# Squares summed on VectorE ahead of one ones-product, and short sequences' new states by 32-row groups

## The reference, cut to what matters

```
k_end = kc * exp(gcum[..., -1:] - gcum)[..., None]
S = S * exp(gcum[..., -1])[..., None, None] + einsum('bhsk,bhsv->bhkv', k_end, u)      # DeltaNet: 4 heads, 128 x 128
...
w_end = exp(gcum[:, -1:] - gcum) * dtc
h = h * exp(gcum[:, -1])[:, :, None, None] + einsum('bsh,bshp,bshn->bhpn', w_end, xc, bc)  # state space: 8 heads, 64 x 128
...
y = y.reshape(bsz, L, MIX_W) * silu(z)
y = y * rsqrt(mean(y * y, axis=-1, keepdims=True) + EPS) * ssd_norm_w      # MIX_W = 512
```

## Time and profile before

| | |
|---|---|
| median of 3 runs | 2747.01 us |
| span of the profiled execution, first to last instruction | 2742.6 us |
| PE busy | 2566.3 us (94%) |
| DVE busy | 1077.8 us (39%) |
| ACT busy | 776.6 us (28%) |
| granted PE clock, mean | 0.981 |

### The profile page before, as it was taken

How to read it: one execution, slowest core, us unless ns; L and a number is a source line. 1 busy time by engine, 2 the same in 40 slices (tenths; PEclk the granted TensorE clock), 3 DMA queues, 4 the chain that set the end, 5 groups by cost and what they waited for, 6 DMA issues and landing times.

```text
span 2742.6 us, 38895 instructions
## 1 busy us (share of the span) xinstructions
PE 2566.3 (94%) x16078; PEld 1550.6 (57%) x16078; DVE 1077.8 (39%) x1748; ACT 776.6 (28%) x1385; POOL 66.4 (2%) x66
## 2 busy tenths in 40 slices
PE   6998999998999999999999999999997899989994
PEld 3555777775555566655555556665446444434443
DVE  4597444544413225553232375752336011101115
ACT  3353323222301111111143118642014122222224
POOL 0000000000000000000000000000000000000003
PEclk9999999999999999999999999999998899999998
DMA  7000122114000011141111210112205656657436
GB/s 307 31 31 34 40 76 102 43 61 158 31 31 31 31 46 57 45 154 63 37 42 50 110 55 33 42 67 120 107 8 197 265 217 241 256 228 287 172 126 223
DMA packets 65269, 291.98 MB, mean 106 GB/s; under 512 B 8956, under 2 KB 32068, under 8 KB 44612
## 3 DMA queue, kind: packets, MB, share of 16 engines
q1 hardware_dynamic: 52996, 255.92, 24.5%
q0 software_dynamic: 8928, 22.03, 2.3%
q10 hardware_dynamic: 3168, 11.54, 1.0%
HBM read 694.20 MB, written 56.63 MB: 274 GB/s over the span
## 4 chain that ended last, share of the span: by engine, by line
PE 81%; DMA 8%; DVE 5%; ACT 4%; issue 2%; SPq 1%; POOL 0%; DVEq 0%; ACTq 0%; POOLq 0%
PE psum L519 30%; PE psum L676 16%; PE psum L1484 8%; DMA arena<-in_moe 6%; PE psum L1342 4%; PE psum L1468 4%; PE psum L1091 2%; PE psum L633 2%; ACT arena L1708 1%; PE psum L537 1%; PE psum L1076 1%; PE psum L563 1%; PE psum L1103 1%; DVE arena L2079 1%; ACT arena L1758 1%
## 5 line engine op out<-in xcount | busy, mean ns | idle before, releaser
L519 PE MATMUL psum<-arena 128*128 128x384 f32 x2544 | 827.1, 488 | 8.1 <-DVEq L321 4.6
L519 PEld LDWEIGHTS psum<-arena 128*128 128x128 f32 x2544 | 485.1, 191 | 347.2 <-issue 9.3
L676 PE MATMUL psum<-arena 128*128 128x384 f32 x1536 | 525.9, 490 | 4.9 <-ACT arena L689 3.3
L676 PEld LDWEIGHTS psum<-arena 128*128 128x128 f32 x1536 | 284.3, 192 | 175.0 <-issue 4.6
L1484 PE MATMUL psum<-arena 128*32 128x256 f32 x5632 | 325.9, 387 | 30.4 <-DMA arena<-in_moe 29.2
L1484 PEld LDWEIGHTS psum<-arena 128*32 128x32 f32 x5632 | 178.9, 112 | 163.6 <-DMA arena<-in_moe 35.2
L1468 PE MATMUL psum<-arena 128*32 128x512 f32 x1408 | 160.7, 594 | 9.9 <-DMA arena<-in_moe 9.3
L1877 ACT ACTIVATE arena<-psum 32x512 f32<-32x512 f32 x176 | 103.4, 588 | 225.1 <-PE psum L1468 223.5
L689 ACT ACTIVATE arena<-psum 128x384 f32<-128x384 f32 x96 | 46.5, 489 | 305.0 <-PE psum L676 251.8
L2537 DVE TENSOR_TENSOR arena<-arena,psum 128x256 f32<-128x256 f32 x44 | 18.5, 422 | 277.3 <-PE psum L1484 187.0
L1342 PE MATMUL psum<-arena 128*128 128x512 f32 (+1 forms) x384 | 126.0, 487 | 0.3 <-issue 0.3
(11 more groups left out here) (514 smaller groups left out, 2689.4 us busy)
## 6 DMA issues: line engine op xcount, KB each, us to landing
arena<-in_moe SPq DMA_DIRECT2D x532, 1024.0 KB
arena<-in_ada SPq DMA_DIRECT2D x12, 2048.0 KB, 8.4
gate_raw<-arena SPq DMA_DIRECT2D x96, 192.0 KB, 1.8
arena<-gate_raw SPq DMA_DIRECT2D x8, 2304.0 KB, 10.8
y_rows<-arena ACTq DMA_DIRECT2D x22, 512.0 KB, 2.9
arena<-in_gate SPq DMA_DIRECT2D x5, 2048.0 KB, 7.7
arena<-in_br SPq DMA_DIRECT2D x4, 2048.0 KB, 8.3
arena<-in_qkv SPq DMA_DIRECT2D x3, 2048.0 KB, 15.2
```

What stands on the lines that cost most here:

```text
L519: last = nc.tensor.matmul(pset(s)[:, n, :], w[:, kk, :], src[:, kk, n * N3:(n + 1) * N3], start=(kk == 0), stop=(kk == K - 1))
L676: last = nc.tensor.matmul(bank(6 + u % 2)[:, 0:N3], w[:, m % 4, kk, :], HT[:, kk, n * N3:(n + 1) * N3], start=(kk == 0), stop=(kk == KD - 1))
```

## The change

Three parts, and a small tile `half` (128 x 2) that marks for every token row whether its sequence is even or odd, made once by DVE ahead of the first DeltaNet chunk.

1. In the state-space norm ACT squares tile m as soon as DVE has gated it (the first square goes straight into the accumulator `acc_s`, which shares its place with `rt_s` and, partly, with `dH`, so that ACT first waits until `ssd_p` is stored). DVE adds the other three squares to it. PE makes 3 products with ones in place of 12, when the last sum is done.
2. In DeltaNet's last chunk the rows are split in 4 groups of 32, each holding two sequences. DVE spreads `cU` over two masked copies (even, odd: 128 x 256). PE makes four products per head, each of 32 rows against 256 columns, one row group per bank 0 to 3. Heads alternate between the halves of a bank. DVE decays ahead of its wait.
3. In the state space's last chunk there are 2 rounds (even, odd) in place of 8. In each round DVE masks `dB` once and decays four states, PE makes 8 products of 32 rows into banks 0, 1, 4 and 5, and DVE adds four. The fills of four sequences stand together ahead of each round's wait.

```diff
@@ PE, DeltaNet's last chunk
-                        for j in range(2):
-                            last = nc.tensor.matmul(bank(j), cKE[:, hs[h]], cUM[:, 512 * j:512 * (j + 1)],
-                                                    start=True, stop=True)
+                        for j in range(4):
+                            r = slice(32 * j, 32 * j + 32)
+                            last = nc.tensor.matmul(bank(j)[:, 256 * (h % 2):256 * (h % 2 + 1)], cKE[r, hs[h]],
+                                                    cUM[r, 256 * (h % 2):256 * (h % 2 + 1)], start=True, stop=True)
                         last.then_inc(c_s, 1)
@@ PE, the state space's last chunk
-                for b in range(NSEQ if sample else 1):
-                    if sample:
-                        fill(c, "b%d" % b)
+                if sample:
+                    for b in range(2):
+                        for q in range(4):
+                            fill(c, "b%d" % (4 * b + q))
                         pe.wait_ge(d_bm, b + 1)
-                    bt = dBM if sample else dB
+                        for g in range(2):
+                            for j in range(4):
+                                r = slice(32 * j, 32 * j + 32)
+                                last = nc.tensor.matmul(bank((0, 1, 4, 5)[j])[:, 256 * g:256 * (g + 1)], dBM[r, g * P:(g + 1) * P],
+                                                        dXW[r, 256 * g:256 * (g + 1)], start=True, stop=True)
+                        last.then_inc(d_s, 1)
...
@@ PE, the norm
-            pe_sumsq(pe, "ssd_ss", 0, sq_s)
+            s, k = FILL[("ssd_ss", 0)]
+            pe.wait_ge(s_free[s], k)
+            pe.wait_ge(s_sq_used, KM - 1)
+            for n in range(3):
+                last = nc.tensor.matmul(pset(s)[:, n, :], ones, acc_s[:, n * N3:(n + 1) * N3], start=True, stop=True)
+            last.then_inc(s_fill[s], 1)
@@ ACT, the norm
-            act.wait_ge(d_gated, 2 * KM)
-            act_sumsq(act, "ssd_ss", 0, sq_s, [XBC[:, m, :] for m in range(KM)])
+            act.wait_ge(s_pstate, 16 * 3)
+            for m in range(KM):
+                act.wait_ge(d_gated, KM + m + 1)
+                if m == 3:
+                    act.wait_ge(s_sq_used, 1)
+                nc.scalar.activation(sq_s[(m - 1) % 2] if m else acc_s, XBC[:, m, :], ACT.Square).then_inc(s_sq, 1)
@@ DVE, ahead of the DeltaNet chunks
+            V.then(nc.vector.reduce_sum(half, c_("row").rearrange("p (j b) -> p b j", b=2), axis=AX.X))
@@ DVE, DeltaNet's last chunk
-                        V.then(tt(hd(cUM, 8), by(cU[:, h * P:(h + 1) * P], 8), over(c_("row"), P), ALU.mult), c_um)
-                        dve.wait_ge(c_s, c + h + 2)
+                        V.then(tt(hd(cUM[:, 256 * (h % 2):256 * (h % 2 + 1)], 2), by(cU[:, h * P:(h + 1) * P], 2), over(half, P),
+                                  ALU.mult), c_um)
                         V.then(tt(S0[:, :, h, :], S0[:, :, h, :],
                                   over(cEG[:, h * P + SLEN - 1:(h + 1) * P:SLEN], P), ALU.mult))
-                        V.then(tt(S0[:, :, h, :], S0[:, :, h, :], hd(psum[:, 0:1024], 8), ALU.add), c_ss)
+                        dve.wait_ge(c_s, c + h + 2)
+                        new = hd(psum[:, 0:2048], 4)[:, :, 256 * (h % 2):256 * (h % 2 + 1)].rearrange("p j (b v) -> p j b v", b=2)
+                        old = S0[:, :, h, :].rearrange("p (j b) v -> p j b v", b=2)
+                        V.then(tt(old, old, new, ALU.add), c_ss)
@@ DVE, the state space's last chunk
-                    for b in range(NSEQ):
-                        V.then(ts(dBM, dB, c_("row", b, 1), None, ALU.mult), d_bm)
+                    for b in range(2):
+                        V.then(ts(dBM, dB, half[:, b:b + 1], None, ALU.mult), d_bm)
+                        for j in range(4):
+                            V.then(tt(H0[:, 2 * j + b], H0[:, 2 * j + b], over(hd(colL, 8)[:, :, 2 * j + b], 64), ALU.mult))
                         dve.wait_ge(d_s, c + b + 1)
-                        V.then(tt(H0[:, b], H0[:, b], over(hd(colL, 8)[:, :, b], 64), ALU.mult))
-                        V.then(tt(H0[:, b], H0[:, b], hd(bank(4), 8), ALU.add), d_ss)
+                        for j in range(4):
+                            V.then(tt(H0[:, 2 * j + b], H0[:, 2 * j + b], hd(bank((0, 1, 4, 5)[j]), 8), ALU.add), d_ss)
@@ DVE, the norm
+            for m in range(1, KM):
+                dve.wait_ge(s_sq, sq_no[("ssd_ss", 0)][m] + 1)
+                V.then(tt(acc_s, acc_s, sq_s[(m - 1) % 2], ALU.add), s_sq_used)
             dve_recip(V, "ssd_ss", 0, rs_s, rt_s)
```

More of the change, by code:

```diff
@@ L391, in build @@
         rs_s, rt_s = cut(Rb + 2 * T, T), cut(Rb + 3 * T, T)
+        acc_s = rt_s
         dDT, dEG = cut(Rb, 1024), cut(Rb + 1024, 1024)
@@ L476, in build @@
         nexpa = small[0:16, 200:201]
+        half = small[:, 202:204]
         S5N = ["dt", "mag", "th", "sin", "cos", "den", "fre", "fim", "t0", "t1", "lre", "lim", "c1", "s1"]
@@ L1216, in _ @@
                 last.then_inc(d_y, 1)
-                for b in range(NSEQ if sample else 1):
-                    if sample:
-                        fill(c, "b%d" % b)
+                if sample:
+                    for b in range(2):
+                        for q in range(4):
+                            fill(c, "b%d" % (4 * b + q))
                         pe.wait_ge(d_bm, b + 1)
-                    bt = dBM if sample else dB
+                        for g in range(2):
[4 more added lines that the diff above has]
+                        last.then_inc(d_s, 1)
+                else:
                     for g in range(2):
-                        last = nc.tensor.matmul(bank(4)[:, 256 * g:256 * (g + 1)], bt[:, g * P:(g + 1) * P],
+                        last = nc.tensor.matmul(bank(4)[:, 256 * g:256 * (g + 1)], dB[:, g * P:(g + 1) * P],
                                                 dXW[:, 256 * g:256 * (g + 1)], start=True, stop=True)
                     last.then_inc(d_s, 1)
-                if not sample:
                     fill(c, "next")
```

## The result

The changed kernel takes 2724.09 us, median of 4 runs (2720.08 to 2729.98), against 2747.34 for the kernel before in the same comparison (4 runs): a ratio of 0.9908, 95% interval 0.989 to 0.9927. Forecast were 2726.6 us and the range 2721.0 to 2732.5. The profiled execution has a span of 2723.2 us, 19.4 less than before (forecast 20.4), and this execution took 2725.01 us, 1.8 above its span. Every run stands 1.7 to 1.9 above its span. So of the 4.4 us that were put down, ahead of the prediction, to what lies before the first and behind the last instruction, only 1.8 are that. The other 2.6 say that the profiled execution of the kernel before was faster than the median, and that is most of why the medians differ by 23.3 us and the two traces by 19.4.

The account below looks back on a forecast made before the run. PE, busy 94% of the span, was taken to bound the kernel; 10.7 + 5.8 + 5.8 - 0.2 - 1.7 = 20.4 us off the 2742.6 span gives 2722.2, with 4.4 added 2726.6 us; range 2721 to 2732.5.

Parts of the forecast that it names:

- Rates: Grouped products in both last chunks: four 32-row records run together, 0.054 us each against 0.215 one at a time.
- The turns: Both last chunks: each switch of PE from full to grouped products or back adds 0.1 us.
- Part 2, 10.7 forecast: DeltaNet's last chunk: ends at 650.9 in place of 661.6, 10.7 us less.
- Head 3 has no fill: DeltaNet's last chunk: the last head's products start at 648.4 without a fill, releasing DVE at 649.1, under the decay.
- one at a time: Rival, chance 0.03: row groups do not overlap; DeltaNet's last chunk gains 6.6 us, the whole change 11.2, time 2735.8.
- The spell behind DeltaNet's chunk, left as it is in the sum: Behind DeltaNet's last chunk: PE's gap shrinks from 3.98 to 3.3 us; the 1.2 GHz stretch's cost, about 2.9, stays.
- The first rival: Fewer slow clock stretches behind the two last chunks, chance 0.27: 2724.9 us without the new one, 2722.0 without either.
- Part 3, 5.8 forecast: State space's last chunk: ends at 1191.2 in place of 1197.05, 5.8 us less.
- The new spell: Behind state space's last chunk: a 3.1 us PE gap brings clock 0.50 for 3.4 us, losing 1.7 (0 to 3.4).
- Part 1, 5.8: State-space norm: 18 fewer records at 0.3225 us save 5.8 us, the sum being ready with 0.7 us to spare.
- given back downstream: Rival, chance 0.05: a transfer becomes late, above all the gates' 2304 KB behind the norm; 2738.2 if 11.6 were lost.
- All that follows shifts whole: Everything behind the changed places, tied by phases to their ends, moves earlier by the full gain, 20.4 us in sum.

Follow-up runs that it names:

- one_group: Changed kernel with all four products of a group reading rows 0 to 31 (one row group): median 2739.66 us, against 2728.37 for the changed kernel.
- decay_late: Changed kernel, but in DeltaNet's last chunk DVE waits for the product ahead of the decay: median 2733.75 us, 5.4 over the changed kernel.
- p2_delta: Kernel before plus only the change to DeltaNet's last chunk (32-row groups): median 2738.68 us, ratio 0.9953 to the kernel before.
- fills_spread: Changed kernel, state space's last chunk with two sequences' fills ahead of each round's wait, four behind the last products: median 2728.34 us, ratio 0.9921 to before.
- spread_stores: Changed kernel with four sequences' state-space fills moved behind the last products and the states' stores sent early: median 2722.92 us, ratio 0.9903 to before.
- p1_norm: Kernel before plus only the norm's change (squares summed on DVE) and the small tile: median 2745.56 us, ratio 0.9982 to the kernel before.
- p3_ssd: Kernel before plus only the change to state space's last chunk (two rounds): median 2745.2 us, ratio 0.9981 to the kernel before.

## Why the prediction was right, step by step

- **Rates: right.** The timeline of the changed kernel, cut to 638.6 to 638.7 us, holds four records' starts in that tenth of a microsecond:

```profile
638.67 0.50 PE L1149 MATMUL psum<-arena 32*128 32x256 f32 x4
```

By the single records these four start at 638.669 to 638.689, and in a steady group the first of each four at 1164.973, 1165.189 and 1165.405: 0.216 us apart. one_group shows what they cost otherwise, 1.99 us for eight. The 3.07 times of the Trainium skill's page "TensorE: Matmul & The Clock Gate", Part 3, is not what this case shows for the steady part. That page gives its number for products of 512 columns; these are of 256. Over a whole group with its turns the ratio is 1.99 to 0.71 for eight records (2.8) and 3.71 to 1.15 for sixteen (3.2), on either side of that number.
- **The turns: too cheap.** I took 0.1 us at each of two. Measured: 0.1 ahead of the group, 0.11 more in its first interval (0.32), 0.11 ahead of the fill (0.32 from the group's last start), 0.1 in the fill's first records. A group costs 0.4 us of turns. In DeltaNet's chunk that is a head of 3.42 in place of 3.2.
- **Part 2, 10.7 forecast, 9.7 measured.** The step that failed is the walk's last head: "Head 3 has no fill". It has one. Its products start at 648.93, and DVE waits 0.48 for them in place of none. That and the turns of the heads ahead of it are the 1.0. The timeline of before would have told it: a fill of 8 records starts at 652.94. decay_late confirms that moving the decay ahead is worth 2.5 of the 9.7, and one_group that the row groups are worth 5.1 (20.1 us for the chunk in place of 15.0). The prediction's price for one at a time, a gain of 6.6 in this chunk, was too kind: one_group's is 4.6. What is left of the 9.7, 2.1 if the shares add, would be the narrower spreading, which no run took away by itself.
- **The spell behind DeltaNet's chunk, left as it is in the sum: wrong, and it helped.** With a gap of 2.75 us the clock stayed at 1.00 in five traces (the changed kernel twice, p2_delta, fills_spread, spread_stores), though with 2.72 (one_group) it fell; with 4.00 (decay_late) and 3.98 (before, p1_norm, p3_ssd) it fell to 0.50 each time, for 6.8 us (before, p1_norm) or 3.4 (p3_ssd, decay_late). The old spell cost 2.9, and that is most of the 3.2 us by which the lead grows from 10.6 to 13.8 where nothing was changed. I had forecast a gap of 3.3, because I let PE stop earlier. The first rival ("or the old one gone") had this half right.
- **`half`, 0.2 forecast, 0.14 measured**, by PE's wait for DVE at DeltaNet's first chunk, before and after:

```profile
274.01 2.07 PE L1060 MATMUL psum<-arena 128*128 128x128 f32 x8 [5.80 <-DVE arena L2054]
```

```profile
273.56 2.08 PE L1062 MATMUL psum<-arena 128*128 128x128 f32 x8 [5.94 <-DVE arena L2073]
```

- **Part 3, 5.8 forecast, 5.4 measured**, the difference being the turns. "Two waits of DVE of about 3.8 and 2.6": 4.25 and 2.87.
- **The new spell, 1.7 with ends at 0 and 3.4: right in kind, too small.** It was 6.8 us long in the changed kernel and cost 2.8 (13.2 us of fill in place of 10.4), 3.4 us long in p3_ssd (1.7). Behind a gap of 3.06 to 3.09 us a spell came in all five traces that have it, behind 0.61 in neither of two (fills_spread, spread_stores). Behind the old 1.62 it came in one of three (p2_delta, not before or p1_norm). So the longer gap makes the spell likelier here; it is not its only cause, and the prediction's "left the clock alone" for 1.62 held for one trace.
- **Part 1, 5.8: right in size**, 1.93 in place of 7.74, and the sum is in time, with the forecast 0.7 us to spare where the clock is full (p1_norm: ready at 1207.19, wanted at 1207.86). That the later chain moves with it is true in the changed kernel; in p1_norm, without the slow spell, PE reaches the stage buffers early and waits 1.58. The rival "given back downstream" was right that a transfer comes late, wrong about which: not the gates' 2304 KB, but the small stores issued behind them and the weights.
- **All that follows shifts whole: nearly.** The lead is 22.2 us at the merge and 19.4 at the end. A part of the difference has its place. PE resumes behind a gap of 2.41 us before and of 2.40 after, and before the clock then stays at 1.00, where after it is 0.50 for 3.4 us (the window at 1699.00 above). Before, gap and window:

```profile
1720.84 4.14 PE L676 MATMUL psum<-arena 128*128 128x384 f32 x12 [2.41 <-ACT arena L689]
```

```profile
1721.00:1724.40 3.40, 3.40 (x11) 2.04 (x12) 3.33 (x4) 0.17 (x1) 0.00 (x0) 1.00 0.31 116
```

After, the gap:

```profile
1698.33 4.22 PE L678 MATMUL psum<-arena 128*128 128x384 f32 x7 [2.40 <-ACT arena L691]
```

The lead falls from 22.5 us there to 20.8 by 1850. What picks the gap stays open. Just ahead of this one stands a gap of 2.86 to 2.88 us, and in each of the ten traces the clock fell behind exactly one of the two: behind the earlier in before and decay_late, behind the later (2.39 to 2.43) in the other eight. The rest of the lead is lost in the experts' part, where slow spells lie elsewhere in every trace, and was not followed up. The runs of one kernel spread over 10 us, so an effect of 1.7 is told by traces, not by medians.

The sum, from the forecast's 20.4 to the lead of 22.2 at the merge: 1.4 less from the chunks (1.0 and 0.4), 1.1 less for the new spell (2.8 in place of 1.7), 2.9 more for the old one, and 0.9 that the changed kernel was ahead already at 635.99. That makes 21.7. Of the 0.5 left over, 0.2 is `half`, which the sum counts and which lies ahead of 635.99, inside the 0.9. Then 2.8 were lost late: 19.4. The 0.9 is chance: up to there the kernels differ by `half` alone, and the same fill starts anywhere from 635.54 to 637.67 in the ten traces. So the mechanism was right in its main terms (the grouped products, the shorter chunks, the norm's products), and that the sum came within 1 us of the traces and 2.5 of the median is luck: 2.9 and 0.9 too little on one side stand against 1.4, 1.1 and 2.8 too much on the other.

## What to carry to other kernels

Where a sum over 128 rows is really four sums over 32, products over 32 rows cost a quarter each in the steady part, issued as here: the four row groups next to one another in order, each into its own bank (no other order or bank was tried). Count about 0.4 us for each change from full products to groups and back. When fills are moved ahead of a wait, look at what stands idle at the loop's end: a gap of 3 us there cost 1.7 to 2.8 us more than itself here, and holding some fills back for behind the last products closes it. When a stretch gets shorter, follow the small stores whose buffers the next stretch needs: here they landed late whenever they were issued right behind large loads, and issuing the loads earlier took 5.4 us off.

## What the runs showed of the hardware

- Behind DeltaNet's last chunk, gaps of PE of 2.72 to 2.75 us left the clock at 1.00 in five traces of six (one_group is the sixth, at 0.50), those of 3.98 to 4.00 were followed by 0.50 four times out of four. The gap's length alone doesn't settle it: at a later place one of 2.41 us was followed by 1.00 before the change, and one of 2.40 by 0.50 after it. Behind 1.62 us the clock fell in p2_delta and stayed in before and p1_norm, behind 2.14 it fell in p1_norm and stayed in before.
- Spells of 1.2 GHz behind a gap of 3.06 to 3.09 us at one place lasted 6.8 us (the changed kernel twice, one_group) or 3.4 us (p3_ssd, decay_late). The same fill of 32 records took 13.2 us up to the next product (the changed kernel twice), 12.4 (one_group) or 12.1 (the other two), where 10.4 is the full clock's.
- Four f32 products of 32 rows against 256 columns, one per row group and each into its own bank, start within 0.02 us, and the next four 0.216 us later; the same in one row group take four times as long, 1.99 us for eight records. Going from full products to a group and back costs 0.4 us.
- The stores of 192 KB land after 1.9 us in the median, but ACT waited 8.8 and 11.0 us for one that was issued right behind 4.8 MB of loads.
